# Two transformer blocks in one kernel on one core: the first operand made pair by pair, and the work at the seams in another order

## Time and profile before

| | |
|---|---|
| median of 3 runs | 2509.72 us (2509.21 to 2511.16) |
| the profiled execution | 2508.24 us, its span 2506.5 us |
| PE busy | 2365.7 us, 94% |
| POOL busy | 2067.3 us, 82% |
| ACT busy | 1048.0 us, 42% |
| DVE busy | 967.2 us, 39% |
| mean granted clock of TensorE | 0.977 |
| loaded | 396.92 MB, 159 GB/s over the span |

### The profile page before, as it was taken

How to read it: one execution, slowest core, us unless ns; L and a number is a source line. 1 busy time by engine, 2 the same in 40 slices (tenths; PEclk the granted TensorE clock), 3 DMA queues, 4 the chain that set the end, 5 groups by cost and what they waited for, 6 DMA issues and landing times. The chain is left out here.

```text
span 2506.5 us, 41868 instructions
## 1 busy us (share of the span) xinstructions
PE 2365.7 (94%) x16709; PEld 2209.4 (88%) x16709; DVE 967.2 (39%) x1434; ACT 1048.0 (42%) x1328; POOL 2067.3 (82%) x1940
## 2 busy tenths in 40 slices
PE   6999998989998899999999999999999998999998
PEld 6989997768997799899898899999999987989876
DVE  5026664553252344022031031632735455245442
ACT  3344445554335333333333333444333334344543
POOL 6988886766785679999999998788997897866576
PEclk9999999999998999999999999999999999999999
DMA  5654444353453445656555655454465456533343
GB/s 180 193 169 149 146 142 126 118 185 118 153 167 118 134 136 185 200 176 194 188 182 189 197 171 182 156 181 156 137 203 168 152 185 190 166 121 118 118 133 119
DMA packets 206872, 401.15 MB, mean 160 GB/s; under 512 B 10498, under 2 KB 20996, under 8 KB 205828
## 3 DMA queue, kind: packets, MB, share of 16 engines
q1 hardware_dynamic: 206724, 399.04, 49.5%
HBM read 396.92 MB, written 2.10 MB: 159 GB/s over the span
## 5 line engine op out<-in xcount | busy, mean ns | idle before, releaser
L594 POOL TENSOR_TENSOR w_low<-ring,w_high 128x512 fp32r<-128x512 f32 (+3 forms) x1872 | 2057.6, 1131 | 416.8 <-ACT w_high L1143 401.6
L1143 ACT ACTIVATE w_high<-ring 128x1024 fp32r<-128x1024 f32 (+2 forms) x760 | 786.8, 1039 | 1325.8 <-PE bank L627 1301.6
L627 PE MATMUL bank<-x_high,w_high 128*128 128x256 f32 x3972 | 1154.6, 291 | 59.7 <-issue 19.7
L627 PE MATMUL bank<-x_low,w_high 128*128 128x256 f32 x3972 | 1136.4, 286 | 0.0
L627 PE MATMUL bank<-x_high,w_low 128*128 128x256 f32 x3972 | 1136.1, 286 | 0.0
L627 PEld LDWEIGHTS bank<-x_high,w_high 128*128 128x128 f32 x3972 | 772.5, 194 | 77.7 <-issue 43.4
L627 PEld LDWEIGHTS bank<-x_low,w_high 128*128 128x128 f32 x3972 | 773.0, 195 | 2.6 <-issue 2.2
L627 PEld LDWEIGHTS bank<-x_high,w_low 128*128 128x128 f32 x3972 | 772.0, 194 | 0.1
L627 PE MATMUL bank<-w_high,hidden 128*128 128x512 f32 x768 | 236.5, 389 | 0.0
L627 PE MATMUL bank<-w_high,x_high 128*128 128x512 f32 x416 | 171.1, 411 | 15.5 <-DVE proj L1664 5.9
L627 PEld LDWEIGHTS bank<-w_high,hidden 128*128 128x128 f32 x768 | 144.0, 188 | 29.7
(11 more groups left out here) (287 smaller groups left out, 1977.8 us busy)
## 6 DMA issues: line engine op xcount, KB each, us to landing
ring<-in_w_in SPq DMA_DIRECT2D x64, 1024.0 KB, 5.5
ring<-in_w_up SPq DMA_DIRECT2D x64, 1024.0 KB, 5.3
ring<-in_w_down SPq DMA_DIRECT2D x64, 1024.0 KB, 5.1
ring<-in_w_out SPq DMA_DIRECT2D x48, 1024.0 KB, 5.1
ring<-in_a_w_in SPq DMA_DIRECT2D x32, 1024.0 KB, 5.1
ring<-in_b_w_in SPq DMA_DIRECT2D x32, 1024.0 KB, 5.2
ring<-in_w_kv SPq DMA_DIRECT2D x24, 1024.0 KB, 5.2
ring<-in_w_mem_kv SPq DMA_DIRECT2D x16, 1024.0 KB, 5.1
```

Source lines behind the costliest of these rows:

```text
L594: last = pool.tensor_tensor(w_low[:, u % UNITS, part], ring[:, u // 2, first:first + n], w_high[:, u % UNITS, part], ALU.subtract)
L627: mm = pe.matmul(out, lhs, rhs, start=start and n == 0, stop=stop and n == 2, skip_group_check=True)
L1143: act.activation(w_high[:, u % UNITS, 0:n], ring[:, u // 2, r0 * g.width:r0 * g.width + n], ACT.Copy)\
```

## The change

At the start, the gains are loaded before the tokens, the tokens come in two loads (512 columns, then after the first weight buffer the rest), and PE turns two pairs of tiles first and one more pair after each of the first six units; the operand is made pair by pair from the banks, ACT and DVE working as for the memories; the squares go to `proj` tiles and are summed before unit 4 of the second block. In the recurrence, ACT does one high part, not two, after the exponential of step 7, and one after step 8. At a seam with a norm, two high parts come before the last square rather than after it, and the sums by columns are made only for the two norms whose products use them. The wait for the turned rows moves from the end of `turned_memory` to the first step of what follows. In `heads` half of the last units' high parts come between logarithms and exponentials, and for the second batch of the mixer's heads the exponentials and the multiplications move in among the next memory's rows. Three attentions leave two units to follow them (`TRAIL`), beside which DVE splits the attention's output; six units in place of four go beside the cross heads. The operand of `cross_out` lies in tiles 8 to 11, and tiles 0 to 7 of the next operand are made between its residuals.

The constants:

```diff
+        FIRST_COLS = 512
         LEAD = 4
+        TURN_UNITS = 2
+        TRAIL = 2
         LEAD_FROM = (0, 0, 0, 1, 2, 2, 3, 4, 4)
+        FIRST_LEAD_FROM = (0, 0, 2, 3, 4, 5, 6, 7, 8)
-        CROSS_HEADS = 8
+        CROSS_HEADS = 10
+        CROSS_Y = 8
```

SyncE; the sixteen gain loads stand where the dots are:

```diff
-            sp.dma_start(tokens, x_rows).then_inc(tokens_in, 16)
...
+            sp.dma_start(tokens[:, :, 0:FIRST_COLS], x_rows[:, :, 0:FIRST_COLS]).then_inc(tokens_in, 16)
                         sp.dma_start(dst, source(n, j)).then_inc(landed[j], 16)
+                        if g.b0 == 0 and isinstance(n, int) and n == 0 and j == 0:
+                            sp.dma_start(tokens[:, :, FIRST_COLS:D], x_rows[:, :, FIRST_COLS:D]).then_inc(tokens_rest_in, 16)
```

TensorE: the start, `norm_sum`, `attend`, the first product, the wait in `heads` and its old place in `turned_memory`, the attentions:

```diff
-            for n in range(KT // 2):
+            for n in range(2):
                 turn_row(n)
...
-                for h in range(TH):
+                for h in range(TH if columns else 0):
...
-            def attend(which, units=()):
+            def attend(which, units=(), trail=()):
                     for name, k in beside:
                         one_unit(name, k)
+                    if n == 0:
+                        pe.wait_ge(rows_kept, turned[0])
...
+                for name, k in trail:
+                    one_unit(name, k)
-            product("hgrn_qf", features_unit, operand, made=x_made["mix"], sums=norm_sum)
+            g = PLAN["hgrn_qf"]
+            for n in range(4):
+                group_free(g.g0 + n)
+                for u in range(8):
+                    if n == 0:
+                        pe.wait_ge(rows_kept, u + 1)
+                    if n == 1 and u == 4:
+                        norm_sum(pair_tile(16, 16), columns=True)
+                    features_unit(g, g.b0 + n, u, pair_of(g.g0 + n), operand, 4 * (u // 2), KT)
+                    if n == 0 and u == 0:
+                        pe.wait_ge(tokens_rest_in, 16)
+                    if n == 0 and u < 6:
+                        turn_row(u + 2)
...
+                        if k == 0:
+                            pe.wait_ge(rows_kept, turned[0])
...
-                pe.wait_ge(rows_kept, turned[0])
...
-            attend(DSA, BESIDE_DSA[LEAD:])
+            attend(DSA, BESIDE_DSA[LEAD:-TRAIL], BESIDE_DSA[-TRAIL:])
-            attend(CROSS, BESIDE_CROSS[CROSS_HEADS:])
+            attend(CROSS, BESIDE_CROSS[CROSS_HEADS:-TRAIL], BESIDE_CROSS[-TRAIL:])
-                features_unit(g, g.b0, u, pair_of(g.g0 + u // 2), operand, 0, 4)
+                features_unit(g, g.b0, u, pair_of(g.g0 + u // 2), lambda kt: operand(CROSS_Y + kt), 0, 4)
-            attend(range(NSA[0], MEM1[-1] + 1), BESIDE_NSA[ROPED:])
+            attend(range(NSA[0], MEM1[-1] + 1), BESIDE_NSA[ROPED:-TRAIL], BESIDE_NSA[-TRAIL:])
```

ScalarE: `high_parts`, `norm_squared`, `heads` after the logarithms of a batch, `rows_high_parts`, the start, the steps of the recurrence:

```diff
                 if root:
-                    high(4)
+                    high(4 - TURN_UNITS)
                     root()
...
                 for c in range(4):
+                    if c == 3:
+                        high(TURN_UNITS)
...
+                    high(last - last // 2)
+                    if first == late:
+                        high(last // 2)
+                        continue
+                    head_exps(batch)
+                    high(last // 2)
-                    act.wait_ge(head_logs, first + BATCH)
-                    for n in batch:
...
-                    high(len(steps[BATCH]))
...
                 for n in range(KT // 2):
+                    if late and n == 3:
+                        head_exps(late)
...
-            high(UNITS)
-            act.wait_ge(rows_kept, 8)
-            norm_squared()
+            act.wait_ge(gains_ready, 1)
+            rows_high_parts(G_MIX, FIRST_LEAD_FROM)
+            for c in range(4):
+                act.wait_ge(rows_kept, 2 * c + 2)
+                act.activation(pair_tile(16 + 4 * c, 4), flat_h(4 * c), ACT.Square).then_inc(norm_squares, 1)
+                high(1)
...
-                    if s < 8:
+                    if s < 7:
                         high(2)
+                    else:
+                        high(1)
```

VectorE: `operand_rows`, the start, and what follows the attentions:

```diff
+            def operand_rows(name, cols, keep_h=False, late=()):
...
+                    if late and n == 4:
+                        for pair in late:
+                            normed_head(pair)
+                    if keep_h:
+                        dve.tensor_copy(flat(hT, 2 * n, 2), bank[5 + m % 3][:, :])
-            keep_rows()
-            operand_of(0, G_MIX)
-            fold()
+            operand_rows("mix", G_MIX, keep_h=True)
+            fold(pair_tile(16, 16))
-            split_tiles("mix_y", (16, 20, 24, 28))
+            for c in range(4):
+                if c == 2:
+                    read_out_ended(BESIDE_DSA[-TRAIL:], places)
+                dve.wait_ge(units_used, 8 * PLAN["mem_v0"].b0 + 2 * c + 2)
+                split_tile_group(16 + 4 * c, c, 4)
-            split_tiles("cross_y", (28,))
-            residual_and_operand("cross_out", 0, G_MLP, lambda u: PLAN["cross_out"].made(3) if u < 2 else 0)
+            dve.wait_ge(units_used, 8 * PLAN["mem_v1"].b0 + CROSS_Y // 2 + 2)
+            split(pair_tile(28, 4), flat(x_high, CROSS_Y, 4), flat(x_low, CROSS_Y, 4)).then_inc(x_ready, 1)
+            read_out_ended(BESIDE_CROSS[-TRAIL:], places)
+            g = PLAN["cross_out"]
+            dve.wait_ge(evacuated, g.g0)
+            for j in range(4):
+                if j == 3:
+                    fold_three(scratch)
+                residual_group("cross_out", j)
+                dve.wait_ge(evacuated, g.g0 + j + 1)
+                if j == 3:
+                    for c in (2, 3):
+                        gained(0, G_MLP, 4 * c, 4).then_inc(x_ready, 1)
+                elif j < 2:
+                    gained(0, G_MLP, 4 * j, 4).then_inc(x_ready, 1)
+            fold_last(scratch)
-            split_gated("nsa_y", 0, ((24, 36, 6), (28, 40, 7), (32, 44, 8), (48, 52, 9)))
+            for c, run in enumerate(((24, 36, 6), (28, 40, 7), (32, 44, 8), (48, 52, 9))):
+                if c == 2:
+                    read_out_ended(BESIDE_NSA[-TRAIL:], places)
+                dve.wait_ge(units_used, 8 * PLAN["nsa_zm"].b0 + 2 * c + 2)
+                split_gated("nsa_y", c, (run,))
```

More of the change, by code:

```diff
@@ L719, in _, with norm_sum @@
             pe.wait_ge(tokens_in, 16)
-            for n in range(KT // 2):
+            for n in range(2):
                 turn_row(n)
             normed = [0]
-            def norm_sum(squares=scratch):
+            def norm_sum(squares=scratch, columns=False):
                 pe.wait_ge(norm_folded, normed[0] + 1)
                 for k in range(4):
-                    pe.matmul(bank[4][:, 0:T], ones[:, :], squares[:, k * T:k * T + T], start=(k == 0),
-                              stop=(k == 3), skip_group_check=True)
-                for h in range(TH):
+                    mm = pe.matmul(bank[4][:, 0:T], ones[:, :], squares[:, k * T:k * T + T], start=(k == 0),
+                                   stop=(k == 3), skip_group_check=True)
+                for h in range(TH if columns else 0):
                     for k in range(4):
@@ L1005, in _ @@
             product("out0", features_unit, lambda kt: operand(4 * GATED_FIRST[kt // 4] + kt % 4), made=x_made["pool_y"])
-            product("cmp_kv", features_unit, operand, made=x_made["kv"], sums=norm_sum)
+            product("cmp_kv", features_unit, operand, made=x_made["kv"], sums=lambda: norm_sum(columns=True))
             swaps = [0]
@@ L1201, in row_squares, with heads @@
                    .then_inc(rows_squared, 1)
-            def heads(pairs, units, rows=None):
+            def heads(pairs, units, rows=None, late=None):
                 for first, steps in batches(pairs, units):
@@ L1212, in heads @@
                         high(len(beside))
+                    last = len(steps[BATCH])
                     for n in batch:
@@ L1339, in _ @@
             rows_high_parts(G_MEM)
-            heads(MIX_PAIRS, BESIDE_MIX_HEADS[LEAD:], MIX_PAIRS[0])
-            rows_high_parts(G_M2A)
-            attend(DSA, BESIDE_DSA[LEAD:])
+            heads(MIX_PAIRS, BESIDE_MIX_HEADS[LEAD:], MIX_PAIRS[0], MIX_PAIRS[BATCH])
+            rows_high_parts(G_M2A, late=MIX_PAIRS[BATCH:])
+            attend(DSA, BESIDE_DSA[LEAD:-TRAIL])
+            high(TRAIL)
             high_parts("mix_out")
@@ L1350, in _ @@
             heads(CROSS_PAIRS, BESIDE_CROSS[LEAD:CROSS_HEADS])
-            attend(CROSS, BESIDE_CROSS[CROSS_HEADS:])
+            attend(CROSS, BESIDE_CROSS[CROSS_HEADS:-TRAIL])
+            high(TRAIL)
             high_parts("cross_out")
@@ L1382, in _ @@
             norm_squared("out0")
-            high_parts("cmp_kv", root)
+            high_parts("cmp_kv", lambda: root(columns=True))
             high_parts("sel_k")
@@ L1413, in _ @@
             high(ROPED)
-            attend(range(NSA[0], MEM1[-1] + 1), BESIDE_NSA[ROPED:])
+            attend(range(NSA[0], MEM1[-1] + 1), BESIDE_NSA[ROPED:-TRAIL])
+            high(TRAIL)
```

(11 more changed lines are left out.)

57 lines of the change are left out of this document (28 added, 29 removed).

## The result

The changed kernel takes 2493.98 us (median of five runs, 2488.17 to 2497.18), the kernel before 2509.72; the ratio is 0.9936 (95% interval 0.9922 to 0.9951). It is faster, but by 15.7 us where 37.4 were forecast, and the time lies outside the forecast range. The profiled execution took 2489.18 us with a span of 2487.4, 19.1 us less than that of before.

The account below looks back on a forecast made before the run. PE was taken to set the pace, its winnable idle time lying in stalls at the seams. Ten terms summed to a 37.4 us gain, 2470.8 us from the profiled 2508.2 and 2472 for the median, range 2457 to 2489.

Parts of the forecast that it names:

- The last attention: Last attention and out1: +2.4 us, +5.5 from the stall behind two units, -3.1 from more steps without a unit.
- Rival C: Many short waits replace few long ones, each followed by half clock; slower, up to 2520 us; chance 0.06.
- Start: First product: +2 us, first unit near 19 us, later units waiting on a ring of turn, high parts and POOL.
- Recurrence: Recurrence's waits at L848: the exponential of step 8 comes earlier, three waits shrink by 0.93 us each; +2.8 us.
- Memories: Products beside the memories: +1 us, cross_k gaining nothing and costing 0.3, mem_k0 net +1.2.
- the cross seam: Cross heads, attention and cross_out: waits go behind units, some steps lack one; +10.4 us.
- `cmp_kv`: The 4.49 us stall leaves unit 4, but nearly 5 us with its clock returns before the sums; +0.4 us.
- `cross_q`: Two high parts come earlier, so PE's 3.63 us stall, its clock and the 1.84 us column sums go; +6.5 us.
- `up0`: First tiles made during cross_out under POOL; the stall stays as long, the column sums' 1.84 us are saved; +1.7 us.
- `pool_qm`: 1.84 us of column sums and 1.4 + 0.45 of POOL waits saved, less 0.6 of fold_last; +3.0 us.
- rival A: The DVE-POOL port lock bites harder, old stalls returning at norm_sum; 14.6 us less gain, 2487 us; chance 0.15.
- rival B: The port lock hardly bites, DVE slipping between POOL's pieces; 13 us more gain, 2459 us; chance 0.12.

Follow-up runs that it names:

- e1: The changed kernel with six bare steps (without a unit) of the last attention moved to steps 8, 14, 20, 26, 32, 38; 2485.39 us.
- e2: The changed kernel with the last attention and the split of out1's operand as in the kernel before; 2484.58 us.
- e4: The changed kernel with three pairs of the first operand turned before the first unit and a first load of 768 columns; 2487.97 us.
- e6: The changed kernel with both units of the recurrence's step 7 cast ahead of the next exponential again, as in the kernel before; 2494.1 us.
- e3: The changed kernel with the 2 MB load of the second memory issued behind cross_v's weight loads, not ahead of them; 2483.51 us.
- e7: The changed kernel with no casts moved ahead of the fourth square in the norms' seams; 2497.01 us.
- e9: The changed kernel with the sums by columns computed in all seams again; 2499.59 us.
- e8: The changed kernel without the two units kept back behind the first two attentions, the last attention keeping its own; 2501.08 us.
- e12: The changed kernel with the last attention's six bare steps in the old phase at uneven distances (6, 9, 18, 24, 33, 36); 2491.07 us.
- e5: The changed kernel with the start of the kernel before: all of x loaded first, eight pairs turned, then the operand made; 2492.79 us.

## Why the prediction was wrong, point by point

**The last attention (+2.4, measured -7.4): the step that failed.** It has two parts. The bare steps were charged with "six or so short waits of 1.3 in place of four of 1.2 (L774), -3.1". Two things were wrong in that. The price came from the steps that were bare before, in another phase of the round; in the phase where the even division puts them now, each waits 1.58 to 1.65 us (5.0 more than the old four, not 3.1). And the rule that waits under 2 us leave the clock alone came from those same four waits, of which one had half clock behind it. Behind the new ones there were five half clocks of 3.41 us, each worth 1.7, four more than before: 6.8 us. One at the start of the attention was 3.41 us long where it had been 6.83 before, which gives 1.7 back. Waits and clock together are 10.1 us, against 10.4 by which `nsa_zq`, `nsa_qm` and `nsa_zm` got longer. e1 and e2 show it from two sides. Rival C had this mechanism, but needed it everywhere, and it struck in one place: the waits of up to 1.25 us at the start, in the attention before `cross_out` and in `cross_out` had the full clock behind them.

The other part, the stall before `out1` with its clock, was put at +5.5, and `out1` got only 2.9 us shorter. The longest wait left in it, 2.02 us for POOL, begins with ScalarE, which stood 5.85 us at the SiLU of `nsa_zm` until VectorE had read it out, with the next high parts behind it:
```profile
2390.75 1.06 ACT L1470 ACTIVATE proj<-proj 128x1024 f32<-128x1024 f32 x1 [5.85 <-DVE proj L1546]
```
VectorE was late with it because two groups of the split stood ahead, made while POOL worked. One of the split's multiplications took 2.30 us there, another 1.21 with POOL idle:
```profile
2383.28 2.30 DVE L1592 TENSOR_TENSOR proj<-proj 128x1024 f32<-128x1024 f32 x1
...
2390.64 1.21 DVE L1592 TENSOR_TENSOR proj<-proj 128x1024 f32<-128x1024 f32 x1
```
No run edits this part by itself.

**Start (+2, measured -0.9).** The working was right in kind: ring, first unit at 19.6 (19 forecast), waits between units, unit 7 at 52.3 (51.4). The later part was mis-sized: unit 15 ended at 80.7, not 77.9, with waits of 0.98 and 0.35 us for GpSimd before units 9 and 10, while VectorE folded the squares. That the folding made GpSimd late is argued, not shown. e4 shows that the ring could be broken.

**Recurrence (+2.8, measured +1.2).** "DVE's operand ... is the next bound. It moves by the same 0.7 to 0.95. So 3 x 0.93": it did not move along. New waits at L865 give back more than L875 saves (e6). The gain that there is comes from the clock, of which the prediction said "that gives little". In e6's trace the three half clocks are there, two more than in the changed kernel's.

**Memories (+1, measured -0.7).** `mem_k0` came out near the forecast in this trace (+1.2, measured +0.9, with `mem_v0` +1.0 besides), but by luck: in half of the traces it takes 42.5 us and loses 1.9 to before. For `cross_k` the prediction named the load that lands at 515.7 and ScalarE behind it, and took the loss at 0.3 us; it was 2.5. The second memory left SP 1.5 us later relative to `cross_k`'s start than before, with a half clock at 491.5 us on the way to its turns, and everything behind the landing moved with it; that the one caused the other is argued, not shown. In most of the other traces `cross_k` took 41 to 42 us, as before (41.5). So this loss is mostly a draw. The stall itself, under both kernels, was worth 7.6 to 9.6 us (e3, against 42 and 44 us), more than the prediction gave to any place but the cross seam.

**`cmp_kv` (+0.4, measured -0.9).** The stall before the sums came back as forecast, at 4.97 us; the casts moved ahead only cost there (e7: 1.0 us, and without them the product is as long as before, 56.1 us).

**Right: `mix_y`, `cross_q`, the cross seam.** 7.9, 7.0 and 10.2 against 7.2, 6.5 and 10.4. In `cross_q` e7 and e9 give 6.2 of casts (with the stall and its clock) and 1.8 of columns, a little over the whole together. Of the cross seam e8 takes apart the trail, 4.5 us; what is left, the wait for the rows and the one for the heads, no run edits by itself. `up0` (+3.2, +1.7 forecast) stalls 4.65 us where 5.7 was expected; its gain is half columns (1.7), none of it casts. `pool_qm` (+2.1, +3.0 forecast) is the columns (1.7) and little more.

**The lock.** Its price is borne out where the forecast used it: `up0` did not start without a stall. By the exclusive lock that the Trainium skill ("SBUF — State Buffer", section "SBUF: two separate sides") states, it would be there at every seam. The traces agree in the earlier trace rows and in the two rows of `out1` above, and a stall reaches PE at `up0` and `cmp_kv`, 4.65 and 4.97 us; at `mix_out` and `cross_q`, behind two units, none does. Of rival A's further losses one came near: it left 2.5 us of the stall's 5.5 at `out1`, and 2.9 were measured. Those at `up0`, `cross_q` and `pool_qm` did not come.

**The range.** Its lower end was set by rival B, its upper by rival A, and both vary the lock. Both move the last attention's stall, and neither its bare steps, where the largest error lay. The condition of C, half clock behind each short wait, was taken as all or nothing; a case "C in the last attention only", six times 1.7 us, would have been worth 10 us, and was not priced. C's own sign, a mean clock not above 0.977, did not come in the profiled execution (0.982), though one of the five runs had 0.976. Three sums do not come out as written, and none of them decides: the parts of the cross seam add to 10.45, not 10.15; B's gains add to 11.0 us, not 13, so 2461; and C lists seventeen places and counts fourteen.

## What to carry to other kernels

When units are divided evenly over the steps of a chain that repeats, look at which step of the round each gap falls on, and price it from that step, not from gaps elsewhere; then move the gaps to the cheap phase, off read-outs and table loads. Price a short wait as a wait and, separately, as a chance of half clock; many equal waits at one distance can nearly all draw the bad lot. And follow a stall that no one edits back to its queue: a 2 MB load issued one place later was worth 7.6 to 9.6 us, where this whole change gave 15.7.

## What the runs showed of the hardware

Waits of PE of 1.6 us were followed by the lower clock level 39 times of 48 where they came 26 to 29 us apart and twice of five in e12; waits of 1.74 and 3.37 us in e1 were followed by the full clock, and waits of 2.2 to 2.3 us in the recurrence by half clock six times of six, in the kernel before and in e6. The kernel before and the changed one had the same waits around 425 us (4.19 and 1.59 before, 4.16 and 1.55 after), yet a half clock of 3.41 us before and of 10.24 us after. Windows of 395 to 490 us, before and after:
```profile
395.00:490.00 95.00, 84.06 (x433) 63.43 (x432) 46.96 (x69) 57.57 (x78) 64.75 (x93) 0.98 0.48 155
```
```profile
395.00:490.00 95.00, 85.36 (x431) 64.76 (x429) 44.71 (x67) 56.81 (x77) 63.51 (x90) 0.95 0.47 155
```
The longer half clock lies around both waits, and `attn_v` lost 1.5 us without an edit. Twelve of the thirteen traces with the changed code there have it; only e5, with the old start, has 3.41 and an `attn_v` of 76.3 us, as before. Whether the start moves it is not shown by one trace. One kernel's times spread over 9 us in five runs, and they follow the granted clock (0.982 to 0.976); that is more than most single edits here are worth.
